# Mixture-of-experts stage of a two-layer diffusion backbone: 32 slots an expert instead of 64, in four column groups

## What is computed

```python
DEPTH = 2
N_GROUPS = 4
EXPERTS_PER_GROUP = 8
TOP_K_IN_GROUP = 2
EXPERT_HIDDEN = D_MODEL // 4
...
    expert_id = g_idx[:, None] * EXPERTS_PER_GROUP + e_idx
    combine = jnp.sum(jax.nn.one_hot(expert_id, N_EXPERTS, dtype=jnp.float32) * e_w[..., None], axis=1)
    a = jnp.einsum('nd,edh->neh', t, w_gate)
    b = jnp.einsum('nd,edh->neh', t, w_up)
    act = jax.nn.silu(a) * b * combine[:, :, None].astype(t.dtype)
    out = jnp.einsum('neh,ehd->nd', act, w_down)
```

## Time and profile before

| what | us |
|---|---|
| median of 3 runs | 1230.47 |
| lowest, highest of the 3 | 1224.69, 1233.09 |
| the profiled execution's own time | 1231.27 |
| its span from first to last instruction | 1229.3 |
| PE busy | 1084.3 (88% of the span) |
| mean granted TensorE clock | 0.966 of full speed |

### The profile page before, as it was taken

One profiled execution on the slowest core, in us unless ns is written; L12 is line 12 of the kernel. 1 busy time (PEld: TensorE's weight loads), 2 busy tenths in 40 slices (PEclk: granted clock), 3 DMA queues, 4 the chain that ended last, 5 costly groups with the idle time before them and its releaser, 6 DMA issues.

```text
span 1229.3 us, 14747 instructions
## 1 busy us (share of the span) xinstructions
PE 1084.3 (88%) x5455; PEld 560.7 (46%) x5455; DVE 478.5 (39%) x1038; ACT 262.0 (21%) x514; POOL 187.9 (15%) x213
## 2 busy tenths in 40 slices
PE   5799978898999879999989999989989878878777
PEld 3344645554444233444445555647945322222224
DVE  2445567326133212332383335777363111111115
ACT  2211244214332121332341111000141011101014
POOL 1020000011322023221110001212013032111210
PEclk8899999999999989999999999999999989998999
DMA  9997895616699965999966020232281599999984
GB/s 349 368 338 284 258 335 225 274 58 246 225 398 404 366 250 197 398 396 401 380 240 229 2 102 1 102 138 84 122 314 66 230 411 413 414 413 408 412 345 154
DMA packets 95585, 330.46 MB, mean 269 GB/s; under 512 B 17546, under 2 KB 33322, under 8 KB 78724
## 3 DMA queue, kind: packets, MB, share of 16 engines
q1 hardware_dynamic: 71936, 303.49, 63.6%
q0 software_dynamic: 16848, 19.29, 4.7%
q10 hardware_dynamic: 6708, 6.45, 1.5%
HBM read 333.22 MB, written 35.35 MB: 300 GB/s over the span
## 4 chain that ended last, share of the span: by engine, by line
PE 60%; DMA 24%; DVE 6%; issue 3%; SPq 3%; ACT 2%; POOL 1%; ACTq 0%; DVEq 0%; POOLq 0%
DMA ring<-in_moe_w_up 14%; PE bank L905 12%; PE bank L1073 10%; PE bank L919 5%; DMA hT<-in_hy_log_decay 4%; PE bank L718 3%; PE bank L1115 3%; PE bank L834 3%; DMA ring<-in_w_ada 3%; PE bank L592 3%; PE bank L1104 2%; PE bank L1059 2%; PE bank L627 2%; DMA work<-token_vectors,curx 2%; PE bank L610 1%
## 5 line engine op out<-in xcount | busy, mean ns | idle before, releaser
L905 PE MATMUL bank<-ring,work 128*64 128x512 f32 x1120 | 262.0, 622 | 45.8 <-DMA ring<-in_moe_w_up 33.8
L905 PEld LDWEIGHTS bank<-ring,work 128*64 128x64 f32 x1120 | 83.1, 143 | 214.0 <-issue 163.5
L919 PE MATMUL bank<-ring,work 128*64 128x512 f32 x560 | 132.2, 615 | 3.6 <-DVE work L1739 1.5
L1073 PE MATMUL bank<-hT,ring 128*128 128x384 f32 x384 | 126.3, 488 | 0.0
L1769 DVE SCALAR_TENSOR_TENSOR work<-bank,work 128x256 f32<-128x256 f32 x32 | 15.5, 484 | 251.7 <-ACT work L1313 242.5
L1073 PEld LDWEIGHTS bank<-hT,ring 128*128 128x128 f32 x384 | 72.2, 190 | 52.0 <-issue 2.3
L919 PEld LDWEIGHTS bank<-ring,work 128*64 128x64 f32 x560 | 38.2, 141 | 76.3 <-issue 66.3
L1786 DVE COPY work<-bank 128x512 f32<-128x512 f32 x32 | 22.1, 691 | 118.3 <-PE bank L919 103.3
L1313 ACT ACTIVATE work<-bank 128x256 f32<-128x256 f32 x32 | 12.2, 383 | 216.5 <-PE bank L905 215.5
L592 PE MATMUL bank<-ring,condS 128*32 128x256 f32 x768 | 47.2, 399 | 9.6 <-DVE ada L1433 5.5
L1938 POOL DMA_INDIRECT work<-token_vectors,work x28 | 28.7, 1023 | 164.9 <-PE bank L888 159.1
(11 more groups left out here) (306 smaller groups left out, 1510.0 us busy)
## 6 DMA issues: line engine op xcount, KB each, us to landing
ring<-in_moe_w_gate SPq DMA_DIRECT2D x32, 2048.0 KB
ring<-in_moe_w_up SPq DMA_DIRECT2D x32, 2048.0 KB
ring<-in_moe_w_down SPq DMA_DIRECT2D x32, 2048.0 KB, 22.7
ring<-in_w_ada SPq DMA_DIRECT2D x24, 2048.0 KB, 13.0
ring<-in_hy_w_in SPq DMA_DIRECT2D x6, 2048.0 KB, 15.3
expert_rows<-work POOLq DMA_DIRECT2D x6, 1024.0 KB, 15.2
filter_spectra<-work ACTq DMA_DIRECT2D x8, 768.0 KB
work<-expert_rows SPq DMA_DIRECT2D x16, 384.0 KB, 7.4
```

What stands on the lines that cost most here:

```text
L905: last = mm(bank[2][WIN * j:WIN * (j + 1), :], gt[:, k, WIN * j:WIN * (j + 1)], gu[:, :, j, k, :], start=(k == 0), stop=(k == KD - 1))
L919: last = mm(bank[b + hf][WIN * j:WIN * (j + 1), :], AT[:, k, WIN * j:WIN * (j + 1)], dn[:, j, k, hf * HALF:(hf + 1) * HALF], start=(k == 0 ...
L1073: last = mm(bank[n % 2][:, 0:T], w[:, k, (n % 4) * P:(n % 4 + 1) * P], hT[:, k, :], start=(k == 0), stop=(k == KD - 1))
```

## The change

A pair now has 64 slots, 32 an expert (`SLOTS`, `WIN`). Each slot's row is split in two halves of 512 features, one on partitions 0 to 63 and one on 64 to 127; rows are fetched and written as halves of 2 KB through `hH` and `yH`. `gate_up` becomes 32 matmuls of 256 columns: the output is cut in two along the hidden size as well, so expert and part give four groups of 32 array columns. `down` becomes 16 matmuls of 256 columns in the same four groups. The tiles `GT`, `S`, `A`, `AT` and the copies of `Y` have half the columns, the turns half the matmuls. Experts with more than 32 tokens now need further rounds: by the counts above pairs 5 (1), 6 (2), 7 (2), 9 (1) and 13 (1) of layer 0, and 0 (2), 1, 2, 4 and 6 (1 each) of layer 1, 13 in all.

`Gx` and `curx` are doubled. POOL fetches the first further rows two pairs ahead; within the loop it fetches the next round's rows (`curn`) as soon as the present ones are turned, and scatters pair q-1 ahead of the loop and not behind it. The slot table is read back in two transfers of 64 partitions, and POOL then adds the half's number to its entries. The filters' rows are issued by ACT behind its copy of `Y` at odd pairs. The diff, cut (`extra` on ACT and DVE changes only its sizes and the numbers it waits for, `xslots` counting two a round):

```diff
--- before.py
+++ after.py
-WIN = 64
+WIN = 32
+SLOTS = 2 * WIN
...
-        Gx = ws(5120, D)
+        Gx = ws(4096, 2 * HALF).rearrange("p (b d) -> p b d", b=2)
-        GT = ws(10240, D).rearrange("p (k s) -> p k s", k=KD)
+        GT = ws(10240, HALF).rearrange("p (k s) -> p k s", k=4)
-        curx = sb("curx", [P, 4], I32)
+        curx = sb("curx", [P, 2, 4], I32)
+        curn = sb("curn", [P, 4], I32)
...
                 load_dn(sp, l, q)
-                if l == 0 and q % 2 == 1:
-                    load_filter(sp, q // 2)
...
                 def gate_up(gt, s, done):
                     gu = slot_gu(s)
                     for k in range(KD):
-                        for j in range(2):
-                            last = mm(bank[2][WIN * j:WIN * (j + 1), :], gt[:, k, WIN * j:WIN * (j + 1)], gu[:, :, j, k, :],
-                                      start=(k == 0), stop=(k == KD - 1))
+                        h, b = divmod(k, 4)
+                        for part in range(2):
+                            for j in range(2):
+                                at = SLOTS * part + WIN * j
+                                last = mm(bank[2][at:at + WIN, 0:2 * P], gt[:, b, SLOTS * h + WIN * j:SLOTS * h + WIN * (j + 1)],
+                                          gu[:, :, j, k, part * P:(part + 1) * P], start=(k == 0), stop=(k == KD - 1))
                     last.then_inc(done, 1)
 
                 def turn_act(done):
-                    for k in range(2):
-                        last = tr(bank[3][:, k * P:(k + 1) * P], A[:, k * P:(k + 1) * P], ident)
-                    last.then_inc(done, 1)
+                    tr(bank[3][:, 0:P], A, ident).then_inc(done, 1)
 
                 def down(s, b, done):
                     dn = slot_dn(s)
                     for hf in range(2):
                         for k in range(2):
-                            for j in range(2):
-                                last = mm(bank[b + hf][WIN * j:WIN * (j + 1), :], AT[:, k, WIN * j:WIN * (j + 1)],
-                                          dn[:, j, k, hf * HALF:(hf + 1) * HALF], start=(k == 0), stop=(k == 1))
+                            for part in range(2):
+                                for j in range(2):
+                                    at, n0 = SLOTS * part + WIN * j, HALF * part + 256 * hf
+                                    last = mm(bank[b + hf][at:at + WIN, 0:256], AT[:, SLOTS * k + WIN * j:SLOTS * k + WIN * (j + 1)],
+                                              dn[:, j, k, n0:n0 + 256], start=(k == 0), stop=(k == 1))
                         last.then_inc(done, 1)
...
                     if l == 0 and q % 2 == 1 and q < PAIRS - 1:
+                        load_filter(act, q // 2 + 1)
                         sizes(q // 2)
...
                 pool.wait_ge(S_("tab_fill"), B_("tab_fill") + 16 * TC * 2)
-                pool.dma_start(tab.rearrange("p (w q) -> p w q", w=NWIN),
-                               tabD[l].rearrange("(w p q) c -> p w (q c)", w=NWIN, p=P)).then_inc(S_("tab_in"), 16)
-                pool.wait_ge(S_("tab_in"), B_("tab_in") + 16)
+                for h in range(2):
+                    pool.dma_start(tab[SLOTS * h:SLOTS * (h + 1), :].rearrange("p (w q) -> p w q", w=NWIN),
+                                   tabD[l].rearrange("(w p q) c -> p w (q c)", w=NWIN, p=SLOTS)).then_inc(S_("tab_in"), 16)
+                pool.wait_ge(S_("tab_in"), B_("tab_in") + 32)
+                places = tab.rearrange("p (n c) -> p n c", c=4)[:, :, 0:2]
+                half = trow[:, TC * 8:TC * 8 + 2].rearrange("p (a c) -> p a c", a=1).to_broadcast([P, NWIN * PAIRS, 2])
+                nc.gpsimd.tensor_tensor(places, places, half, ALU.add).then_inc(S_("g_clear"), 1)
...
                 def scatter(q):
                     pool.wait_ge(S_("y_set"), B_("y_set") + 2 * (q + 1))
-                    ind(out=yD, out_offset=at_rows(tab[:, 4 * q:4 * q + 1]), in_=Y[:, q % 2, :], in_offset=None,
-                        bounds_check=2 * T - 1, oob_is_err=False).then_inc(S_(f"scat{q % 2}_"), 16)
+                    ind(out=yH, out_offset=at_rows(tab[:, 4 * q:4 * q + 1]), in_=Y[:, q % 2, :], in_offset=None,
+                        bounds_check=4 * T - 1, oob_is_err=False).then_inc(S_(f"scat{q % 2}_"), 16)
...
                     with pool.If(hi > lo):
                         with pool.Fori(lo, hi) as x:
+                            pool.wait_ge(S_("xgt_mm"), x + 1)
+                            apart(pool)
+                            at = further(((x - lo + 2) * PAIRS + q) * 4, NWIN * PAIRS * 4 - 4)
+                            nc.gpsimd.tensor_copy(curn[:, :], tab[:, bass.ds(at, 4)]).then_inc(S_("xslots"), 1)
+                            pool.wait_ge(S_("xslots"), 2 * x + 2)
+                            apart(pool)
+                            ind(out=Gx[:, q % 2, :], out_offset=None, in_=hH, in_offset=at_rows(curn[:, 1:2]),
+                                bounds_check=2 * T - 1, oob_is_err=False).then_inc(S_("xgath"), 16)
                             pool.wait_ge(S_("xy_set"), 2 * (x + 1))
                             apart(pool)
-                            ind(out=yD, out_offset=at_rows(curx[:, 0:1]), in_=Yx, in_offset=None,
-                                bounds_check=2 * T - 1, oob_is_err=False).then_inc(S_("xscatter"), 16)
+                            ind(out=yH, out_offset=at_rows(curx[:, q % 2, 0:1]), in_=Yx, in_offset=None,
+                                bounds_check=4 * T - 1, oob_is_err=False).then_inc(S_("xscatter"), 16)
                             pool.wait_ge(S_("xscatter"), 16 * (x + 1))
                             apart(pool)
-                            at = further(((x - lo + 2) * PAIRS + q) * 4, NWIN * PAIRS * 4 - 4)
-                            nc.gpsimd.tensor_copy(curx[:, :], tab[:, bass.ds(at, 4)]).then_inc(S_("xslots"), 1)
-                            pool.wait_ge(S_("xslots"), x + 2)
+                            pool.wait_ge(S_("xgath"), 16 * (x + 2))
                             apart(pool)
-                            ind(out=Gx, out_offset=None, in_=hD, in_offset=at_rows(curx[:, 1:2]),
-                                bounds_check=T - 1, oob_is_err=False).then_inc(S_("xgath"), 16)
-                            pool.wait_ge(S_("xgath"), 16 * (x + 2))
+                            nc.gpsimd.tensor_copy(curx[:, q % 2, :], curn[:, :]).then_inc(S_("xslots"), 1)
+                            pool.wait_ge(S_("xslots"), 2 * x + 3)
+                            apart(pool)
 
                 def second(q):
                     apart(pool)
                     if l + q > 0:
                         pool.wait_ge(S_("xnext_in"), 16 * (l * PAIRS + q))
-                    nc.gpsimd.tensor_copy(curx[:, :], tab[:, (PAIRS + q) * 4:(PAIRS + q) * 4 + 4]).then_inc(S_("xnext"), 1)
+                    nc.gpsimd.tensor_copy(curx[:, q % 2, :], tab[:, (PAIRS + q) * 4:(PAIRS + q) * 4 + 4]).then_inc(S_("xnext"), 1)
                     pool.wait_ge(S_("xnext"), l * PAIRS + q + 1)
-                    ind(out=Gx, out_offset=None, in_=hD, in_offset=at_rows(curx[:, 1:2]),
-                        bounds_check=T - 1, oob_is_err=False).then_inc(S_("xnext_in"), 16)
+                    ind(out=Gx[:, q % 2, :], out_offset=None, in_=hH, in_offset=at_rows(curx[:, q % 2, 1:2]),
+                        bounds_check=2 * T - 1, oob_is_err=False).then_inc(S_("xnext_in"), 16)
...
                 second(0)
+                second(1)
                 for q in range(PAIRS):
-                    extra(q)
-                    if q + 1 < PAIRS:
-                        second(q + 1)
                     apart(pool)
-                    if q == PAIRS - 1:
-                        nc.gpsimd.nop().then_inc(S_("rows_done"), 1)
                     if q >= 1:
                         scatter(q - 1)
                     if l == 0 and q % 2 == 0 and q >= 2:
                         size_sums(q // 2 - 1)
+                    extra(q)
+                    if q + 2 < PAIRS:
+                        second(q + 2)
+                    apart(pool)
+                    if q == PAIRS - 1:
+                        nc.gpsimd.nop().then_inc(S_("rows_done"), 1)
                     if 1 <= q and q + 3 < PAIRS:
                         pool.wait_ge(S_("gt_mm"), B_("gt_mm") + 2 * (q + 2))
                         gather(q + 3)
```

147 lines of the change are left out of this document (77 added, 70 removed).

## The result

| kernel | median us | lowest, highest | runs |
|---|---|---|---|
| before, timed beside it | 1231.78 | 1224.69, 1233.91 | 4 |
| the changed kernel | 1268.19 | 1265.31, 1275.62 | 4 |

The changed kernel takes 1.0315 times as long, interval 1.0254 to 1.0377: 36 us more by the medians, where 6 less were forecast, and outside the range. Its profiled execution took 1265.3 us, span 1263.5, which is 34.2 us above the span of before. A ratio leaves out executions well above the fastest of their kernel, so it can differ from the quotient of the medians (most for b_halfrows).

The account below looks back on a forecast made before the run. Weight transfers were taken as the bound, saturated in layer 1, with 29 us idle in layer 0. Pauses 0, start -1.5, end -7.0, layer 1 +0.9, rows +1.5 gave -6.1 us: 1224 us, range 1204 to 1248.

Parts of the forecast that it names:

- The two products: Each pair: `gate_up` 3.6 us for 7.0, `down` 1.8 for 3.65; 170 us over 32 pairs, worth nothing in themselves.
- Rival (3): Four groups not side by side behind a striding operand: `gate_up` stays at 7 us, total about 1248; chance 0.03.
- Layer 0's pauses: Layer 0's weight stream: 7 us at pair 6, 20 at pair 7, 2 here and there; 29 in all, unchanged.
- price of a second round under load: Further rounds: a second one takes 14.4 us under load, its multiply waiting for the scatter of the round before.
- Layer 0's start: Up to pair 2's first weights: pair 0's shorter products, held by the slot table's wait, keep 1.5 of 5.3 us.
- Layer 1's start: Stream start after pair 0's further rounds: later by 5.7 us, with second table transfer, POOL's sum and two rounds.
- split read of the slot table: Table read in two transfers: costs one issue, 1.0 us, or also part of a second landing, at most 3.2.
- Rows of 2 KB: Same bytes in some 3,072 more packets: +1.5 us, at most 8, at least 0.
- The two ends: Layer 0's end -7.0 us (7.8 for 14.8); layer 1's -5.8, 2 lost if the rows' transfer is not ready first.
- what remains behind the last down weights: Layer 0's end: a 2 MB transfer (5.2 us), the rows' first quarter (2 us), a sum of 0.6; 7.8 us.
- The stages behind: Both layers' sum stages: the prediction gave them no term, 0 us.
- Rival (2): TensorE stays at low clock in rounds and `gate_up` behind waits, layer 0 pairs 5-9, layer 1 0-4: about 1260; chance 0.20.

Follow-up runs that it names:

- b_halfrows: Kernel before, with the product adding pair 15's rows taking only the first 64 of its 128 partitions; 1244.0 us, ratio 1.0077.
- a_sums: a_fullrows, with VectorE adding only the first quarter of the rows read back ahead of pair 15's copy into Y, the second behind it; 1236.8 us, ratio 1.0050.
- b_best: Kernel before with the change's order and ACT's filter rows, 64 slots an expert, plus the VectorE edit of a_sums; 1218.8 us, ratio 0.9909.
- a_fullrows: Changed kernel, with the product adding pair 15's rows taking all 128 partitions again, zeros for the unwanted half; 1239.7 us, ratio 1.0090.
- a_all64: Changed kernel, with the products adding the other pairs' rows also on 64 partitions, so the whole sum stage has one height; 1255.9 us, ratio 1.0194.
- a_norounds: a_fullrows without any further rounds, tokens beyond an expert's 32nd left out; 1175.8 us, ratio 0.9583.

## Why the prediction was wrong, and where it was right

- **The two products.** Right: 3.66 and 1.93 us, worth nothing in themselves where the stream is the bound. Rival (3), that the four groups do not run side by side, fell with them.
- **Layer 0's pauses.** The sum was right (28 us for 29), its parts were not: 11 us at pair 6 (430 to 444), 13 at pair 7 (460 to 480), 3 at pair 9 (510 to 520), for 7, 20 and 2 here and there, so the nearness of the sum is in part luck. The price of a second round under load was wrong (10.5, not 14.4), and so was its reason: the multiply's last wait was for ACT or, once and by 0.1 us, for the entries behind the scatter.
- **Layer 0's start: -1.5 forecast, +1.9 measured.** "Pair 0's products are shorter" was counted as a gain, though the multiply waits for the table. The timeline of after shows the table last, at 314.15, 1.26 us later than the multiply of before (312.89); TensorE had idled 4.3 us by then, and `down` came at the low clock, 3.64 us for 1.93. The shorter `gate_up` had taken away the cover.
- **Layer 1's start: +5.7 forecast, +4.8 measured.** Right in the sum. The split read of the slot table cost less than its one issue: from issue to use 4.5 us, for 4.2 before, so neither the 1.0 us nor a part of a second landing shows; GpSimd's sum behind it took 1.7 with its wait, for 1.4.

```profile
952.19 1.74 POOL L1942 DMA_DIRECT2D work<-slot_table  x2 [1.43 <-DMA slot_table<-pay,idx]
956.68 0.87 POOL L1947 TENSOR_TENSOR work<-work,trow 128x416 int32<-128x416 int32 x1 [2.75 <-DMA work<-slot_table]
```

- **Rows of 2 KB: +1.5 forecast, not measured.** No run parts this term from the rest. Its premise, more packets, does not show either: the page of after has 12,368 packets on q0, for 16,848 before; why they are fewer is open.
- **The two ends: -7.0 and -5.8 forecast, -1.1 (with the rest of the layer) and -0.7 measured.** With -1.1 and -0.7 for -5.5 and -4.8 of the table's stretches, 8.5 us of the miss are here. What failed is the list of "what remains behind the last down weights": a transfer ahead of the rows and their first quarter. What remains, as the timeline of after reads, is pair 14's scatter (issued 608.2, landed by 614.5), the rows read back behind it, and two quarters of sums on VectorE ahead of the copy of pair 15: the copy went at 624.96, its product had ended at 622.74. a_sums and b_best bear on the last of these alone. In layer 1 I had named the rows' transfer as the cover, at 2 us; 4 were lost.
- **The stages behind: 0 forecast, +26.5 measured.** This is the step that made the prediction wrong: it took the two sum stages as unchanged, without a reason. They were not, since `last_rows` takes 64 partitions now, which the prediction never priced. The runs showed 24.2 and 23.8 us for 10.8 each: the level, lost behind the longer wait, came back with 128 rows (a_fullrows, 12.4 and 12.2 us) and not with 64 (a_all64). Rival (2) had TensorE at its low level and 1260, but for another place, the rounds and `gate_up` of pairs 5 to 9, and for another length, the start behind each wait; that its time came so near to 1268 is luck. In the place that it named the loss was small: of the rounds of pairs 6 and 7, only the first `gate_up` of pair 6 was slow (5.45 us), and the windows over the pauses above have the clock at 1.00. a_norounds adds that a mean clock of 0.83 costs nothing where the stream is the bound.
- a_fullrows takes this term out and runs at 1.0090 of before, where -6 us would be 0.995. What is left between, some 17 us, is by the profiled executions the two starts and ends above (11), the 3 us of low clock at the head of the two stages, and layer 0, which in that execution took 336.6 us from the rows written to the sum stage (333.5 in the changed kernel's). These last 3 us I can't place.

The Trainium skill, "TensorE: Matmul & The Clock Gate", Part 1, describes the clock as gated by how busy the array has been, so that sustained work brings it back. The 128-row stage of a_fullrows agrees: back within 4 us. The stages with 64 rows do not: busy without a break for 18.6 to 25.3 us and still at 0.50. The measurement decides.

## What to carry to other kernels

When a change makes TensorE wait more, price the first stage that is bound by TensorE behind the waits, not just the waiting products: it may be entered at the low clock, and here only work that uses the array's full height brought the clock back. Price every matmul whose shape changes, also where its columns and count do not; padding half-height operands with zeros to 128 rows added no matmul and gave 28 us back (23 of them in the two stages). And where a stream is the bound, a faster product buys nothing, while extra serial rounds that hold a ring place cost: here 13 of them 64 us.

## What the runs showed of the hardware that I had not expected

- The granted clock does not follow busy time alone. With products of 64 of the 128 rows in the stage, TensorE kept the high level in three stages (13.7 us at 1.00). In the five where the level was low at the entry or fell in the first 2 us it did not regain it (18.6 to 25.3 us, busy throughout). With 128 rows it did in all seven such stages, within 3 to 6 us.
- A change between products of 64 and 128 rows cost about 0.2 us each at full clock: the weight load no longer ran beside the matmul in front of it (1.71 us a turn of the loop for 1.32).
- Two transfers of 64 partitions for one of 128 cost 0.3 us from issue to use with this small table (4.5 for 4.2), though their issue took 1.74 us for 1.00.
- An indirect scatter had landed 2.8 us behind its issue in an idle stretch (DMA share 0.10), against 9.8 under the stream; the two do not write the same rows.
